# Own buffers for the normed input of the feed-forwards and the second mixer, at chosen byte offsets

## The chip, the cores and the metric

One core of a Trainium2 chip runs the whole program in one launch. The metric is device time in microseconds (us); lower is better.

## What is computed

The reference runs a hybrid block and then two further layers on x of 256 tokens by 1024 features, all in float32:

```
x = x + hybrid_mixer(rmsnorm(x))            # norm 0
x = x + swiglu(rmsnorm(x))                  # norm 2, first feed-forward
x = rmsnorm(x)
x = x + hgrn2_mixer(rmsnorm(x))             # norm 3, second mixer
x = x + swiglu(rmsnorm(x))                  # norm 5, second feed-forward
x = x + rglru_mixer(rmsnorm(x))             # norm 6, third mixer
x = x + swiglu(rmsnorm(x))                  # norm 7, third feed-forward
out = rmsnorm(x)                            # norm 8

swiglu(h) = (silu(h @ w_gate) * (h @ w_up)) @ w_down      # 1024 -> 2816 -> 1024
```

The numbers are those by which the kernel calls its norms (`e`). Norms 1 and 4 are not norms of x: they stand for the inputs of the first two mixers' output products, which have buffers of their own (`eh`, `el`).

## The kernel before, in words

**Weights.** Every weight matrix is cut into units of 1 MB (2048 fp32 columns per partition). SyncE loads units into a ring of three slots, `raw`. ScalarE copies a unit in two halves, rounded, to `whi` (`split`, L983), and VectorE, or GpSimd for the second halves in the feed-forwards, subtracts to get the remainder `wlo` (L1389, L2012). The activations are split in the same way: `hh` and `hl` for a normed input, `gh` and `gl` for the gated product inside a feed-forward, `bh` and `bl` for a branch of the first mixer, `ch` and `cl` in the third mixer. Every product is three matmuls: high by high, low weight by high, high weight by low.

**Two forms of product.** `still` (L507, L510, L515) has a 128x128 block of the weights as stationary operand and 256 columns of the activation, all tokens, as moving operand. It serves `project_columns` and `project_pair`. `moving` (L527, L531, L535) has a 128x128 block of the activation as stationary operand and 512 columns of the weights as moving operand. It serves `project_tokens` and `add_product`. In both forms each matmul has a load of its own stationary block (PEld), and the load for the next matmul runs beside the present one.

**A feed-forward** (`feed_forward(f, e, e2)`) first makes gate and up projections from `hh` and `hl`: 22 units of 48 `still` matmuls, 1056 in all. Two of these units are in `project_pair`, which mixes them with transposes; the rest follow one another. Then `add_product` multiplies `gh`, `gl` by the down weights: 11 units of 24 `moving` matmuls. During its last unit TensorE transposes the next normed input into PSUM (`transposes`, L577), ScalarE copies it to `hh` and VectorE writes the remainder to `hl` (both in functions named `turned`).

**The second mixer** makes 8 `still` units (`hf`, `hq`, 384 matmuls) and then 8 `moving` units (`hv`, `hg`, 24 matmuls each, 192 in all) from `hh` and `hl`, with smaller matmuls of its own between them.

**The order of the work** is written out by hand per engine; every engine waits on semaphores that count what others have finished. A wait is on data, not on a tensor's name.

**Where tensors lie.** Tensors lie one behind the other in a partition in the order of their declarations; stages that follow each other reuse the space behind `gap_stage`. A 128-column stationary block of fp32 is 512 bytes, and all blocks of a tensor begin at a multiple of 512 bytes from the tensor's start. So a tensor's distance from `whi` modulo 512 bytes, called its place here, is the same for all its blocks. From the sizes declared: `whi` and `wlo` have place 0; `hh` and `hl` lie behind `gap_hh` of 32 bytes and have place 32; `eh`, `el` are declared without that gap and have place 0; `gap_stage` brings the stage tensors back to place 0, so `gh` and `gl` have place 0; `gap_bh` gives `bh` and `bl` place 64; `gap_ch` gives `ch` and `cl` place 0.

```
sbuf(root, "gap_hh", [128, 8])
hh = sbuf(root, "hh", [128, 8, 256], f32r)
hl = sbuf(root, "hl", [128, 8, 256], f32r)
```

Of the kernel before, what the change touches and what calls it, by code (L numbers as in the profile page):

```python
# [8 lines left out]
f32 = mybir.dt.float32  # L9
f32r = mybir.dt.float32r  # L10
i32 = mybir.dt.int32
ACT = mybir.ActivationFunctionType
# [62 lines left out]
def build(nc, a):  # L75
    V, A, G, T, S = nc.vector, nc.scalar, nc.gpsimd, nc.tensor, nc.sync
    vq, aq, gq, tq, sq = Waits(V), Waits(A), Waits(G), Waits(T), Waits(S)
    with ExitStack() as root:
# [3 lines left out]
        def sbuf(ctx, name, shape, dt=f32):  # L82
            return ctx.enter_context(nc.sbuf_tensor(name, shape, dt))
# [12 lines left out]
        hh = sbuf(root, "hh", [128, 8, 256], f32r)  # L96
        hl = sbuf(root, "hl", [128, 8, 256], f32r)
# [32 lines left out]
        ffn = []  # L130
        for f in range(3):
            ctx = ExitStack()
            ffn.append((sbuf(ctx, f"gh_{f}", [128, 22, 256], f32r), sbuf(ctx, f"gl_{f}", [128, 22, 256], f32r),
                        sbuf(ctx, f"sg_{f}", [128, 2, 512]), sbuf(ctx, f"bc_f{f}", [128, 256])))
            ctx.close()

        hg = ExitStack()
# [10 lines left out]
        nw = sbuf(hg, "nw", [128, 128])  # L148
        mstat = sbuf(hg, "mstat", [128, 16])
        bc_hg = sbuf(hg, "bc_hg", [128, 256])  # L150
        hg.close()

        lr = ExitStack()
# [10 lines left out]
        bc_lr = sbuf(lr, "bc_lr", [128, 256])  # L164
        gw = sbuf(lr, "gw", [128, 2, 4, 512])
        lr.close()

        def two(ap):
            return ap.rearrange("p (k t) -> p k t", k=2)
# [203 lines left out]
        def bank_of(*key):  # L373
            return banks[turns[key][0]]
# [113 lines left out]
        def tensor_program():  # L488
# [49 lines left out]
            def of_norm(e):  # L538
                return (lambda k: hh_set(e, k)), (lambda k: hl_set(e, k))

            def project_columns(key, e, between=None):
                j = unit_at[key]
                b = turn(("col", *key), next_bank())
                tq.wait_ge(*free(("col", *key)))
                for m in range(units[j][2] // 128):
                    t = still(banks[b][:, 256 * m:256 * m + 256], j, m, hh, hl, range(8), *of_norm(e))
                    if between is not None and m == 0:
                        between()
                t.then_inc(s_full[b], 1)
                used[j, 0] = used[j, 1] = full("col", *key)  # L550

            def project_tokens(key, e, between=None):
                bs = [turn(("tok", *key, 0), next_bank()), turn(("tok", *key, 1), next_bank(), 2)]
                for part in range(2):
                    j = unit_at[(*key, part)]
                    for t in range(2):
                        if part == 0:
                            tq.wait_ge(*free(("tok", *key, t)))
                        tok = moving(banks[bs[t]][:, :], j, t, hh, hl, range(4 * part, 4 * part + 4), 0, 512, *of_norm(e),
                                     first=part == 0, last=part == 1)  # L560
                        if t == 1 or part == 1:
                            tok.then_inc(s_full[bs[t]], 1)
                    b, _, n = turns["tok", *key, 1]
                    used[j, 0] = used[j, 1] = (s_full[b], n - 1 + part)
                    if between is not None:
                        between(part)
# [21 lines left out]
            def project_pair(keys, e):  # L588
                js = [unit_at[key] for key in keys]
                bs = [turn(("col", *key), next_bank(), 2) for key in keys]  # L590
                for part in range(2):
                    for i, j in enumerate(js):
                        for m in range(2):
                            if part == 0:
                                tq.wait_ge(*free(("col", *keys[i])))
                            tok = still(banks[bs[i]][:, 256 * m:256 * m + 256], j, m, hh, hl, range(4 * part, 4 * part + 4),
                                        *of_norm(e), i0=4 * part, first=part == m == 0, last=part == m == 1,
                                        inside=(lambda: spread_factors(e)) if part == i == 1 and m == 0 and e == 3 else None)
                        tok.then_inc(s_full[bs[i]], 1)
                        used[j, part] = (s_full[bs[i]], turns["col", *keys[i]][2] - 1 + part)  # L600
                        if part == i == 0:
                            transposes(1, e)
                        if part == 1 and i == 0 and e != 3:
                            spread_factors(e)
# [367 lines left out]
        def scalar_program():  # L972
# [38 lines left out]
            def turned(c, e):  # L1011
                for n in range(2):
                    q = 2 * c + n
                    aq.wait_ge(*full("tr", e, q))
                    A.activation(hh[:, 2 * q:2 * q + 2, :], two(bank_of("tr", e, q)[:, :]), ACT.Copy).then_inc(s_hh, 1)

            def project_pair(keys, e, bc, evacs):
                j = unit_at[keys[0]]
# [189 lines left out]
            add_product(("wo",), 4, 2)  # L1208

            def feed_forward(f, e, e2, again=None):  # L1210
                gh, gl, sg, bc = ffn[f]

                def gate_of(j):
                    aq.wait_ge(*evac("col", "g", f, j))
                    A.activation(sg[:, j % 2, :], sg[:, j % 2, :], ACT.Silu).then_inc(s_silu, 1)  # L1215

                def up_of(j):
                    aq.wait_ge(*evac("col", "u", f, j))
                    A.activation(gh[:, 2 * j:2 * j + 2, :], two(sg[:, j % 2, :]), ACT.Copy).then_inc(s_gh, 1)  # L1219

                project_pair([("g", f, 0), ("u", f, 0)], e, bc, [lambda: gate_of(0), lambda: up_of(0)])
                for j in range(1, 11):
                    use(("g", f, j))
                    gate_of(j)
                    use(("u", f, j))
                    up_of(j)
                    if f == 0 and j == 2:
                        aq.wait_ge(s_arg, 2)
                        A.activation(cst[:, 1:3, :], cst[:, 1:3, :], ACT.Exp).then_inc(s_exp, 1)
                    if f == 0 and j == 4:  # L1230
                        aq.wait_ge(s_arg, 3)
                        A.activation(cst[:, 0, :], cst[:, 0, :], ACT.Exp).then_inc(s_exp, 1)
                add_product(("down", f), 11, e2, e2 == 8, again=again)
# [143 lines left out]
        def vector_program():  # L1377
# [30 lines left out]
            def turned(c, e):  # L1408
                for n in range(2):
                    q = 2 * c + n  # L1410
                    sl = slice(2 * q, 2 * q + 2)
                    vq.wait_ge(*hh_set(e, 2 * q))
                    V.tensor_tensor(hl[:, sl, :], two(bank_of("tr", e, q)[:, :]), hh[:, sl, :].bitcast(f32),
                                    ALU.subtract).then_inc(evacuated("tr", e, q), 1)

            def spread_factor(e):
# [340 lines left out]
            series = [None]  # L1757

            def feed_forward(f, e, e2, again=None):
                gh, gl, sg, bc = ffn[f]  # L1760

                def gate_of(j):
                    if j >= 2:
                        vq.wait_ge(s_gl, 11 * f + j - 1)
                    scaled(two(sg[:, j % 2, :]), ("g", f, j), e, bc)

                def up_of(j):
                    s = sg[:, j % 2, :]
                    vq.wait_ge(s_silu, 11 * f + j + 1)
                    vq.wait_ge(*full("col", "u", f, j))  # L1770
                    V.tensor_tensor(s, s, bank_of("col", "u", f, j)[:, :], ALU.mult).then_inc(evacuated("col", "u", f, j), 1)  # L1771
                    vq.wait_ge(s_gh, 11 * f + j + 1)
                    V.tensor_tensor(gl[:, 2 * j:2 * j + 2, :], two(s), gh[:, 2 * j:2 * j + 2, :].bitcast(f32), ALU.subtract).then_inc(s_gl, 1)  # L1773

                project_pair([("g", f, 0), ("u", f, 0)], e, [lambda: gate_of(0), lambda: up_of(0)])
                for j in range(1, 11):
                    use(("g", f, j))
                    gate_of(j)
                    use(("u", f, j))
                    up_of(j)  # L1780
                    if f == 0:
                        constants(j)
                if again is not None:
                    vq.wait_ge(*row_ready(3))
                    vq.wait_ge(*row_ready(4))
                    own_row = own.mark(V.tensor_tensor(wrow[:, 0, :], wrow[:, 1, :], wrow[:, 0, :], ALU.mult))
                    vq.wait_ge(*own_row)
                add_product(("down", f), 11, e2, e, e2 == 8, again=again)
# [488 lines left out]
```

## Time and profile before

| | us |
|---|---|
| median of 3 runs (lowest to highest) | 1131.96 (1131.92 to 1132.42) |
| the profiled execution: its time | 1132.61 |
| the profiled execution: its span | 1131.4 |
| TensorE busy, of the span | 1116.7 |
| gate and up projections of one feed-forward, unbroken part | 114.89 |

A busy share of TensorE says that some matmul was in flight, not how fast matmuls follow each other. For that, read start times: the distance between two rows of the timeline, divided by the matmuls between them. It is called the interval below.

### The profile page before, as it was taken

How to read it: one execution, taken by the hardware profiler on the slowest of the kernel's cores; microseconds unless marked ns; L12 is line 12 of the kernel's file. 1: busy time of each engine (PE TensorE's matmuls, PEld its weight loads, DVE VectorE, ACT ScalarE, POOL GpSimd, SP SyncE). 2: the span in 40 equal slices, each digit the busy share in tenths (PEclk: the TensorE clock that was granted, in tenths of full speed). 3: DMA queues.
4: the chain of work that ended last, by engine and by line, in shares of the span. 5: the costliest groups of instructions: out<-in, count | busy, mean ns of one | idle time of the engine just before them, and what ended most of it. 6: DMA issues, size and time to landing. Idle time of an engine off the chain costs nothing.

```text
span 1131.4 us, 19249 instructions
## 1 busy us (share of the span) xinstructions
PE 1116.7 (99%) x8085; PEld 1039.6 (92%) x8085; DVE 658.0 (58%) x1052; ACT 571.3 (51%) x866; POOL 291.6 (26%) x193
## 2 busy tenths in 40 slices
PE   8999999999999999999999999999999999999997
PEld 6899989999989999889998889999889979999986
DVE  6755755677676454338897565343238897434324
ACT  6646555555455644436642545444335855544432
POOL 3022100000005445422311215444510003444440
PEclk9999999999999999999999999999999999999999
DMA  8689474544646666664545358665555254666551
GB/s 266 206 250 335 138 239 150 162 155 137 211 157 208 189 185 203 199 196 142 169 130 169 112 160 274 210 190 190 193 180 188 92 184 151 219 190 188 189 184 38
DMA packets 155088, 207.25 MB, mean 183 GB/s; under 512 B 9471, under 2 KB 128409, under 8 KB 155002
## 3 DMA queue, kind: packets, MB, share of 16 engines
q1 hardware_dynamic: 151274, 193.11, 54.1%
q0 software_dynamic: 3728, 12.92, 3.5%
q8 instruction: 64, 1.05, 0.4%
q14 instruction: 22, 0.18, 0.0%
HBM read 204.78 MB, written 4.24 MB: 185 GB/s over the span
## 4 chain that ended last, share of the span: by engine, by line
PE 81%; DVE 12%; ACT 4%; issue 1%; DMA 1%; POOL 0%; SPq 0%; DVEq 0%; ACTq 0%
PE bank L507 16%; PE bank L510 16%; PE bank L515 16%; PE bank L535 9%; PE bank L531 9%; PE bank L527 9%; DVE wlo L1389 4%; ACT whi L983 1%; PE bank L888 1%; PE bank L802 1%; PE bank L812 1%; DVE area L1537 1%; DMA raw<-in_w_in 1%; PE bank L577 1%; PE bank L824 1%
## 5 line engine op out<-in xcount | busy, mean ns | idle before, releaser
L1389 DVE TENSOR_TENSOR wlo<-raw,whi 128x1024 fp32r<-128x1024 f32 x275 | 336.0, 1249 | 240.0 <-ACT whi L983 239.2
L983 ACT ACTIVATE whi<-raw 128x1024 fp32r<-128x1024 f32 x362 | 360.8, 1045 | 116.0 <-PE bank L535 100.7
L2012 POOL TENSOR_TENSOR wlo<-raw,whi 128x1024 fp32r<-128x1024 f32 x87 | 222.7, 2560 | 250.8 <-ACT whi L983 250.8
L507 PE MATMUL bank<-hh,whi 128*128 128x256 f32 x1784 | 284.3, 281 | 0.0
L515 PE MATMUL bank<-hl,whi 128*128 128x256 f32 x1784 | 281.3, 279 | 0.0
L510 PE MATMUL bank<-hh,wlo 128*128 128x256 f32 x1784 | 281.2, 279 | 0.0
L507 PEld LDWEIGHTS bank<-hh,whi 128*128 128x128 f32 x1784 | 240.6, 188 | 2.1 <-issue 1.4
L510 PEld LDWEIGHTS bank<-hh,wlo 128*128 128x128 f32 x1784 | 239.9, 188 | 0.0
L515 PEld LDWEIGHTS bank<-hl,whi 128*128 128x128 f32 x1784 | 239.7, 188 | 0.0
L2019 POOL TENSOR_TENSOR st<-st,half 128x1 f32<-128x1 f32 x18 | 10.3, 582 | 335.0 <-DVE st L1406 302.1
L527 PE MATMUL bank<-whi,gh 128*128 128x512 f32 x264 | 81.5, 390 | 0.0
L535 PE MATMUL bank<-whi,gl 128*128 128x512 f32 x264 | 81.3, 389 | 0.0
L531 PE MATMUL bank<-wlo,gh 128*128 128x512 f32 x264 | 81.3, 389 | 0.0
L1215 ACT ACTIVATE sg<-sg 128x512 f32<-128x512 f32 x33 | 20.9, 633 | 94.2 <-DVE sg L1436 94.2
L1219 ACT ACTIVATE gh<-sg 128x512 fp32r<-128x512 f32 x33 | 20.8, 632 | 84.1 <-DVE sg L1771 84.1
L535 PEld LDWEIGHTS bank<-whi,gl 128*128 128x128 f32 x264 | 49.6, 188 | 10.4
L531 PEld LDWEIGHTS bank<-wlo,gh 128*128 128x128 f32 x264 | 49.6, 188 | 10.3
L527 PEld LDWEIGHTS bank<-whi,gh 128*128 128x128 f32 x264 | 49.2, 188 | 9.9
L1771 DVE TENSOR_TENSOR sg<-sg,bank 128x512 f32<-128x512 f32 x33 | 22.7, 688 | 55.6 <-PE bank L515 53.5
L1436 DVE TENSOR_TENSOR sg<-bank,bc_f 128x512 f32<-128x512 f32 x33 | 22.8, 690 | 45.4 <-PE bank L515 45.4
L1008 ACT ACTIVATE bank<-x_sb 128x512 f32<-128x512 f32 x26 | 15.6, 600 | 57.7 <-DVE x_sb L1458 29.9
L1773 DVE TENSOR_TENSOR gl<-sg,gh 128x512 fp32r<-128x512 f32 x33 | 30.7, 931 | 23.3 <-ACT gh L1219 23.3
(318 smaller groups left out, 1214.7 us busy)
## 6 DMA issues: line engine op xcount, KB each, us to landing
raw<-in_ffn_w_in SPq DMA_DIRECT2D x88, 512.0 KB, 3.8
raw<-in_w_in SPq DMA_DIRECT2D x72, 512.0 KB, 4.8
raw<-in_ffn_w_out SPq DMA_DIRECT2D x44, 512.0 KB, 3.3
raw<-in_hgrn_w_in SPq DMA_DIRECT2D x32, 512.0 KB, 4.0
raw<-in_w_ffn_gate SPq DMA_DIRECT2D x22, 512.0 KB, 4.4
raw<-in_w_ffn_up SPq DMA_DIRECT2D x22, 512.0 KB, 4.4
raw<-in_w_ffn_down SPq DMA_DIRECT2D x22, 512.0 KB, 3.3
raw<-in_w_branch SPq DMA_DIRECT2D x16, 512.0 KB, 4.4
```

The source lines that it names most:

```text
L507: T.matmul(out, wh[:, i, c], xh[:, k, :], start=first and (i, k) == pairs[0], stop=False)
L510: T.matmul(out, wl[:, i, c], xh[:, k, :], start=False, stop=False)
L515: t = T.matmul(out, wh[:, i, c], xl[:, k, :], start=False, stop=last and (i, k) == pairs[-1])
L527: tok = T.matmul(out, xh[:, k, r], wh[:, i, c], start=first and i == 0, stop=False)
L531: tok = T.matmul(out, xh[:, k, r], wl[:, i, c], start=False, stop=False)
L535: tok = T.matmul(out, xl[:, k, r], wh[:, i, c], start=False, stop=last and i == len(ks) - 1)
L983: A.activation(half_of(whi, j, h), half_of(raw, j, h), ACT.Copy).then_inc(s_hi[j % NS][h], 1)
L1389: V.tensor_tensor(half_of(wlo, j, h), half_of(raw, j, h), half_of(whi, j, h).bitcast(f32), ALU.subtract).then_inc(s_lo[j % NS][h], 1)
L1436: V.tensor_tensor(dst, two(bank_of("col", *key)[:, :]), bc[:, :].rearrange("p (o t) -> p o t", o=1).broadcast_to([128, 2, 256]), ALU.mult) ...
L1771: V.tensor_tensor(s, s, bank_of("col", "u", f, j)[:, :], ALU.mult).then_inc(evacuated("col", "u", f, j), 1)
L1773: V.tensor_tensor(gl[:, 2 * j:2 * j + 2, :], two(s), gh[:, 2 * j:2 * j + 2, :].bitcast(f32), ALU.subtract).then_inc(s_gl, 1)
L2012: G.tensor_tensor(half_of(wlo, j, 1), half_of(raw, j, 1), half_of(whi, j, 1).bitcast(f32), ALU.subtract).then_inc(s_lo[j % NS][1], 1)
```

## The change

Normed inputs 2, 3, 5 and 7 get tensors of their own in place of `hh`, `hl`. `NORMED[e]` names the pair for every norm; norms 0 and 6 keep `hh`, `hl`. `normed_at(t, byte)` takes the high half `byte` bytes behind the tensor's start and the low half 8192 bytes behind that. By the sizes, `normed_f` begins at place 0, so the pairs of the feed-forwards have places 48, 16 and 0; `gap_normed` of 192 bytes gives the second mixer's pair place 0. The readers (`project_columns`, `project_tokens`, `project_pair`) and the two writers (`turned`) go through `NORMED[e]`.

```diff
             ffn.append((sbuf(ctx, f"gh_{f}", [128, 22, 256], f32r), sbuf(ctx, f"gl_{f}", [128, 22, 256], f32r),
-                        sbuf(ctx, f"sg_{f}", [128, 2, 512]), sbuf(ctx, f"bc_f{f}", [128, 256])))
+                        sbuf(ctx, f"sg_{f}", [128, 2, 512]), sbuf(ctx, f"bc_f{f}", [128, 256]),
+                        sbuf(ctx, f"normed_{f}", [128, 4096 + 16], f32r)))
...
         bc_hg = sbuf(hg, "bc_hg", [128, 256])
+        sbuf(hg, "gap_normed", [128, 48])
+        normed_hg = sbuf(hg, "normed_hg", [128, 4096], f32r)
...
+        def normed_at(t, byte):
+            return tuple(t[:, byte // 4 + 2048 * i:byte // 4 + 2048 * i + 2048].rearrange("p (k t) -> p k t", k=8) for i in range(2))
+
+        NORMED = {0: (hh, hl), 2: normed_at(ffn[0][4], 48), 3: normed_at(normed_hg, 0), 5: normed_at(ffn[1][4], 16),
+                  6: (hh, hl), 7: normed_at(ffn[2][4], 0)}
...
-                    t = still(banks[b][:, 256 * m:256 * m + 256], j, m, hh, hl, range(8), *of_norm(e))
+                    t = still(banks[b][:, 256 * m:256 * m + 256], j, m, *NORMED[e], range(8), *of_norm(e))
...
-                        tok = moving(banks[bs[t]][:, :], j, t, hh, hl, range(4 * part, 4 * part + 4), 0, 512, *of_norm(e),
+                        tok = moving(banks[bs[t]][:, :], j, t, *NORMED[e], range(4 * part, 4 * part + 4), 0, 512, *of_norm(e),
...
-                            tok = still(banks[bs[i]][:, 256 * m:256 * m + 256], j, m, hh, hl, range(4 * part, 4 * part + 4),
+                            tok = still(banks[bs[i]][:, 256 * m:256 * m + 256], j, m, *NORMED[e], range(4 * part, 4 * part + 4),
...
-                    A.activation(hh[:, 2 * q:2 * q + 2, :], two(bank_of("tr", e, q)[:, :]), ACT.Copy).then_inc(s_hh, 1)
+                    A.activation(NORMED[e][0][:, 2 * q:2 * q + 2, :], two(bank_of("tr", e, q)[:, :]), ACT.Copy).then_inc(s_hh, 1)
...
-                    V.tensor_tensor(hl[:, sl, :], two(bank_of("tr", e, q)[:, :]), hh[:, sl, :].bitcast(f32),
+                    V.tensor_tensor(NORMED[e][1][:, sl, :], two(bank_of("tr", e, q)[:, :]), NORMED[e][0][:, sl, :].bitcast(f32),
                                     ALU.subtract).then_inc(evacuated("tr", e, q), 1)
```

## Rows read from the trace of the kernel before

**Rows 1.** The page: span, busy time of TensorE, granted clock and GB/s in 40 slices.
```profile
span 1131.4 us, 19249 instructions
PE 1116.7 (99%) x8085; PEld 1039.6 (92%) x8085; DVE 658.0 (58%) x1052; ACT 571.3 (51%) x866; POOL 291.6 (26%) x193
...
PEclk9999999999999999999999999999999999999999
...
GB/s 266 206 250 335 138 239 150 162 155 137 211 157 208 189 185 203 199 196 142 169 130 169 112 160 274 210 190 190 193 180 188 92 184 151 219 190 188 189 184 38
```

**Rows 2.** The page's groups: the three matmuls of `still` on `hh` and `hl`.
```profile
L507 PE MATMUL bank<-hh,whi 128*128 128x256 f32 x1784 | 284.3, 281 | 0.0
L515 PE MATMUL bank<-hl,whi 128*128 128x256 f32 x1784 | 281.3, 279 | 0.0
L510 PE MATMUL bank<-hh,wlo 128*128 128x256 f32 x1784 | 281.2, 279 | 0.0
```

**Rows 3.** Windows, unbroken gate and up stretches of the three feed-forwards; columns named above.
```profile
core 0: us, PE busy (x) PEld busy (x) DVE busy (x) ACT busy (x) POOL busy (x), PEclk, DMA share, GB/s
342.73:457.62 114.89, 114.89 (x988) 114.89 (x987) 57.03 (x77) 60.23 (x71) 54.78 (x22) 1.00 0.64 194
679.24:794.12 114.88, 114.88 (x987) 114.88 (x986) 51.52 (x52) 53.42 (x64) 53.16 (x22) 1.00 0.67 213
950.40:1065.29 114.89, 114.89 (x988) 114.89 (x986) 51.53 (x52) 54.71 (x65) 53.18 (x22) 1.00 0.63 195
```

**Rows 4.** Timeline of PE, first feed-forward: start us, us, instructions; begin and end.
```profile
342.73 0.71 PE L507 MATMUL bank<-hh,whi 128*128 128x256 f32 x4
343.28 0.63 PE L510 MATMUL bank<-hh,wlo 128*128 128x256 f32 x4
...
457.15 0.63 PE L515 MATMUL bank<-hl,whi 128*128 128x256 f32 x4
457.62 0.64 PE L527 MATMUL bank<-whi,gh 128*128 128x512 f32 x2
```

**Rows 5.** Timeline of PE, `moving` with stationary `hh`, `hl` (second mixer).
```profile
604.45 1.17 PE L527 MATMUL bank<-whi,hh 128*128 128x512 f32 x4
605.46 1.09 PE L531 MATMUL bank<-wlo,hh 128*128 128x512 f32 x4
...
609.19 1.10 PE L535 MATMUL bank<-whi,hl 128*128 128x512 f32 x4
610.12 0.60 PE L884 MATMUL bank<-qT,kT 128*128 128x128 f32 x4
```

**Rows 6.** Timeline of PE, `moving` with stationary `gh`, `gl`, second feed-forward (all pairs of two).
```profile
800.04 0.62 PE L531 MATMUL bank<-wlo,gh 128*128 128x512 f32 x2
...
835.40 0.62 PE L531 MATMUL bank<-wlo,gh 128*128 128x512 f32 x2
```

**Rows 7.** Timeline of PE, `still` with moving `bh`, `bl`: third branch, then fourth.
```profile
260.65 0.39 PE L510 MATMUL bank<-bh,wlo 128*128 128x256 f32 x2
...
271.07 0.39 PE L515 MATMUL bank<-bl,whi 128*128 128x256 f32 x2
...
300.02 0.40 PE L510 MATMUL bank<-bh,wlo 128*128 128x256 f32 x2
...
310.15 0.40 PE L515 MATMUL bank<-bl,whi 128*128 128x256 f32 x2
```

**Rows 8.** Timeline of PE: the 64 matmuls of the third mixer's gates, plain fp32.
```profile
878.64 14.08 PE L954 MATMUL bank<-uc,gw 128*128 128x256 f32 x64
892.37 0.82 PE L507 MATMUL bank<-hh,whi 128*128 128x256 f32 x4
```

**Rows 9.** Windows, second mixer: the `still` part, then the `moving` part.
```profile
522.50:576.50 54.00, 53.84 (x455) 53.64 (x452) 47.58 (x89) 35.40 (x43) 21.24 (x33) 1.00 0.49 155
576.50:645.00 68.50, 68.08 (x395) 58.89 (x395) 51.04 (x100) 26.07 (x52) 7.88 (x8) 1.00 0.48 154
```

**Rows 10.** Chain that ended last, second mixer: start us, us, what (longest pieces).
```profile
550.81 2.27 DVE wlo L1389 x2
560.65 1.21 DVE wlo L1389
565.63 2.27 DVE wlo L1389 x2
...
607.48 0.93 PE bank L527 x4
608.42 0.93 PE bank L531 x4
609.35 0.93 PE bank L535 x4
```

More of the change, by code:

```diff
@@ L1210, in feed_forward @@
             def feed_forward(f, e, e2, again=None):
-                gh, gl, sg, bc = ffn[f]
+                gh, gl, sg, bc, _ = ffn[f]
                 def gate_of(j):
@@ L1759, in feed_forward @@
             def feed_forward(f, e, e2, again=None):
-                gh, gl, sg, bc = ffn[f]
+                gh, gl, sg, bc, _ = ffn[f]
                 def gate_of(j):
```

## The prediction

> **What bounds the kernel now.** I read the page first: TensorE is busy for 1116.7 of 1131.4 us, at the full granted clock (2.4 GHz level) in every slice [rows 1]. So time can only come from how fast its matmuls follow each other, or be lost there. The groups show where most of them are: three times 1784 matmuls of one form with the normed input as moving operand [rows 2]. Their mean of 280 ns is flight time and says nothing of pace, so I went to the timeline for intervals. In the first feed-forward 984 `still` matmuls run from 342.73 to 457.62 without a break: 114.89 / 984 = 116.8 ns each [rows 4], and the other two stretches take the same 114.88 and 114.89 us [rows 3]. In them VectorE works 45 to 50%, ScalarE 46 to 52% and GpSimd 46 to 48% of the time, and DMA 63 to 67% [rows 3]: nothing else is near its limit.
>
> **Is 116.8 ns what such a matmul must take?** Two comparisons say no, and both differ from it in where the operands lie. First, the `moving` form: with stationary `hh`, `hl` (place 32) 16 matmuls run from 605.46 to 609.19, 233.1 ns each [rows 5]; with stationary `gh`, `gl` (place 0) 156 run from 800.04 to 835.40, 226.7 ns each [rows 6]. Same form, same moving tensors, same slots; 6.4 ns apart. Second, the `still` form on `bh`, `bl` (place 64), same shape as in the feed-forwards: 92 matmuls from 260.65 to 271.07 are 113.3 ns apart, and 86 from 300.02 to 310.15 are 117.8 ns apart [rows 7]. So one place can give two steady paces, each held to the end of its stretch, with starts that differ in what ran just before.
>
> I read this as two streams out of the same memory, the moving operand and the next stationary block, that get into each other's way as often as their distance and their relative timing make them; a pace once found repeats. In the same trace a plain fp32 product of 256 columns keeps (892.37 - 878.64) / 64 = 214.5 ns [rows 8]. It reads its moving operand for about twice as long, so it is no bound for this form.
>
> The Trainium skill speaks against any effect: "TensorE: Matmul & The Clock Gate", Part 2, step by step, says that TensorE has two independent read ports and that loading the next weights does not take read bandwidth from the running matmul. The trace does not agree: 233.1 against 226.7 ns, with only the stationary tensor changed. By that rule the sum below would be zero.
>
> **The change part by part.**
>
> *Instructions.* None is added, removed or moved: the two writers and three readers get other addresses. ScalarE still makes 4 copies per norm and VectorE 4 subtractions, on the same semaphores. No wait goes either, since the old readers of `hh` were done long before it was written again. No DMA is touched. Cost: nothing, and nothing has to cover it.
>
> *Second mixer, `moving` part.* 8 units of 24, 192 matmuls, go from place 32 to place 0, which is exactly the case of rows 6: 192 x (233.1 - 226.7) = 1.2 us. Here TensorE is the chain in most pieces [rows 10], and VectorE works 51.0 of 68.5 us [rows 9], so I count the whole of it. Bounds: 0, if VectorE's or ScalarE's waits take it up, and 1.2.
>
> *Second mixer, `still` part.* 384 matmuls, place 32 to 0. No row shows `still` at place 0. The nearest is place 64: between -3.5 and +1.0 ns each against 116.8, so -1.3 to +0.4 us. VectorE works 47.6 of 54.0 us there [rows 9] and its `wlo` pieces alternate with TensorE in the chain [rows 10]; what is late next is `wlo`. I take 0.
>
> *The feed-forwards.* 3 x 1056 = 3168 `still` matmuls go from place 32 to 48, 16 and 0. This is the term that decides, and no row shows these places in this form. Lower bound: the pace of 113.3 ns, the quickest of this form, 3.5 ns less per matmul, 3.7 us per feed-forward, 11.1 us in all. Upper bound: 117.8 ns, 1.0 ns more, 1.1 us per feed-forward, 3.3 us in all. I take the lower bound for all three. The reason is rows 5 and 6: place 0 is quicker than 32 in the `moving` form by 6.4 ns, and the `still` form has as moving operand half as many columns; half of 6.4 is 3.2, near the 3.5 between 116.8 and 113.3. For places 48 and 16 that is weaker: they lie between the two seen, and a steady pace halfway, 115.0, would give half the gain there. I do not take halfway because all rows show paces held, not blends.
>
> Is the rest quick enough? A unit would take 48 x 113.3 = 5.44 us in place of 5.60. The down product already uses a 1 MB unit up in 24 x 226.7 = 5.44 us [rows 6], from the same ring, and DMA would have to bring 1 MB in 5.44 us, 193 GB/s, as it does now on average [rows 3], where slices up to 335 GB/s are seen [rows 1]. GpSimd's share, 54.8 us in 114.9, would become 49%. So the cover stands.
>
> *Sum.* 11.1 + 1.2 + 0 = 12.3 us. The profiled execution took 1132.61 us, of which 1131.4 are span and 1.2 lie around it, untouched. That execution stands 0.65 above the median of 1131.96, so the median goes to 1131.96 - 12.3 = **1119.7 us**.
>
> **The rivals.**
>
> *A: all three feed-forwards find the quick pace.* 1119.7. Chance 0.47.
>
> *B: one or two of them do.* Place 64 has both paces in the same trace, so what ran just before a stretch seems to choose [rows 7]. Two quick and one as now: 8.6 us less, 1123.4. One quick, two at 117.8: 3.7 + 1.2 - 2.2 = 2.7 us less, 1129.3. Against it: each stretch starts in the same way, behind the same transposes. Chance 0.25.
>
> *C: place does not matter for these stretches.* This is the skill's rule at work, or paces that depend on timing alone. Then either nothing changes, 1132.0, or only the `moving` part gains, 1130.8. All three at 117.8 belongs here by its size: 3.3 - 1.2 = 2.1 us more, 1134.1. For the rule: three stretches with three different neighbours agree to 0.01 us [rows 3]. Against it: rows 5, 6 and 7. Chance 0.12.
>
> *D: the new places are worse.* Place: the 3168 feed-forward matmuls. If places 16 and 48 put the two streams into step, so that each matmul loses 3 ns more than now, half of what separates rows 5 and 6, the price is 3168 x 3 = 9.5 us, less 1.2: 1140.3. It decides from 117.9 ns on: (117.9 - 116.8) x 3168 = 3.5, less 1.2, is 2.3 us, 0.2% of the time. For it: 117.8 has been seen at another place. Against it: nothing slower is held over a whole stretch in these rows. Chance 0.10.
>
> *E: quicker than any row.* If 16 or 48 parts the two streams altogether, the gain could go beyond 3.5 ns; twice that in two stretches would be 7.4 us more, 1112.3. Chance 0.06.
>
> **How the numbers follow.** 0.2% is 2.3 us, about what a measurement of this kernel can tell from no change. A, B and E lie below 1129.7, though B at its weak end only just: I count 0.77 for faster. C is within 0.2%, with the weak end of B: 0.13. D is slower: 0.10. The range leaves out D and half of E, and takes in A, B and the gaining half of C: 1114 to 1131.
>
> **What would show it.** In the new trace I would divide the three unbroken stretches by 984: 111.5 us for A, 114.9 for C, 116 or more for D. The three need not agree; if they differ, B is right and the place or the start decides. The second mixer's token units should take 24 x 226.7 = 5.44 us in place of 5.67 (604.45 to 610.12, where the next group starts [rows 5]). Shares of the other engines should rise only because the stretch is shorter, and no wait of TensorE for `wlo` or `whi` should appear inside it. The prediction is wrong if places 48 and 16 hold a pace that is neither 113.3 nor near it, or if TensorE starts to wait for the weights' halves at 5.44 us a unit.

## The result and the profile after

The change made the kernel slower: 1137.15 us median of 5 runs (1136.67 to 1137.53), against 1132.06 before (1131.92 to 1132.43). The ratio is 1.0042, 95% interval 1.0031 to 1.0053. Forecast were 1119.7 us and a range of 1114 to 1131.

First the page of the kernel after, its first two lines:

```profile
span 1135.8 us, 19249 instructions
PE 1121.9 (99%) x8085; PEld 1046.4 (92%) x8085; DVE 658.5 (58%) x1052; ACT 571.4 (50%) x866; POOL 291.0 (26%) x193
```

The instructions are as many as before; the span is 4.4 us longer and TensorE is busy for 5.2 us more [rows 1]. Next the windows of the kernel after (columns as in [rows 3]): the three unbroken stretches of gate and up projections, then the second mixer from its first product with the normed input to its last.

```profile
342.48:459.00 116.52, 116.52 (x987) 116.52 (x986) 56.97 (x77) 60.26 (x71) 54.69 (x22) 1.00 0.65 192
680.22:795.10 114.88, 114.88 (x987) 114.88 (x986) 51.53 (x52) 53.42 (x64) 53.47 (x22) 1.00 0.67 213
951.51:1069.67 118.16, 118.16 (x987) 118.16 (x986) 51.57 (x52) 54.65 (x65) 53.38 (x22) 1.00 0.62 189
519.78:642.30 122.52, 122.30 (x850) 114.10 (x849) 101.94 (x193) 60.11 (x89) 26.96 (x39) 1.00 0.51 159
```

The stretches were 114.9 us each [rows 3]. Place 48 now takes 1.6 us more, place 16 nothing more, and place 0 takes 3.3 us more. Divided by 984 matmuls, the paces are 118.4, 116.8 and 120.1 ns. TensorE is busy through the whole of each stretch, the profile lists no wait of it there, and the other engines' busy times stand still: its own pace changed.

The second mixer was 122.99 us (518.45 to 641.44) and is 122.52. In it, one `moving` unit in the timeline of PE, and below it one `still` unit, both of the kernel after; the last two rows are begin and end of that `still` unit in the kernel before:

```profile
605.91 1.17 PE L536 MATMUL bank<-whi,normed_hg 128*128 128x512 f32 x4
606.91 1.07 PE L540 MATMUL bank<-wlo,normed_hg 128*128 128x512 f32 x4
...
610.54 1.07 PE L544 MATMUL bank<-whi,normed_hg 128*128 128x512 f32 x4
611.45 0.60 PE L893 MATMUL bank<-qT,kT 128*128 128x128 f32 x4
...
570.32 0.77 PE L516 MATMUL bank<-normed_hg,whi 128*128 128x256 f32 x4
...
576.20 0.56 PE L897 MATMUL bank<-qT,kT 128*128 128x64 f32 x4
...
568.18 0.77 PE L507 MATMUL bank<-hh,whi 128*128 128x256 f32 x4
...
573.97 0.44 PE L888 MATMUL bank<-qT,kT 128*128 128x64 f32 x3
```

The `moving` unit takes 611.45 - 605.91 = 5.54 us, where it took 5.67 [rows 5]; the `still` unit takes 5.88, where the same one took 5.79. The `moving` units gain about 1.0 us over all eight, and the `still` units give back about 0.9 (46.9 us for their 384 matmuls, 46.0 before), so the two nearly cancel. That the window is 0.5 us shorter comes mostly from two waits of TensorE of 0.2 us each that the kernel before has and the kernel after has not:

```profile
PE bank L585 <- DVE diag L1419: 0.2, 1, 0.2
PE bank L869 <- DVE Ss L1846: 0.2, 1, 0.2
```

They do not follow the place: with the places of before, `e1_place32` below has one of them and `e8_all_moved` neither.

With the pieces ahead of each stretch, from the first projection to the down product, the feed-forwards stand at +1.7 (126.28 from 124.54), +0.1 and +3.4 us (128.01 from 124.59), the second mixer at -0.5. The program's start came 0.4 us earlier. The sum is +4.4 us, the whole difference of the spans.

### The profile page after: what moved, and what is told of

Same layout as the page of the kernel before. It is cut to its first block, busy times and chain, and to the rows that moved or that the text cites. A ratio compares the mean times of both kernels' runs of the same rounds, so it can differ in the third digit from the quotient of the medians.

```text
span 1135.8 us, 19249 instructions
## 1 busy us (share of the span) xinstructions
PE 1121.9 (99%) x8085; PEld 1046.4 (92%) x8085; DVE 658.5 (58%) x1052; ACT 571.4 (50%) x866; POOL 291.0 (26%) x193
## 4 chain that ended last, share of the span: by engine, by line
PE 87%; DVE 8%; ACT 3%; issue 1%; DMA 0%; SPq 0%; POOL 0%; DVEq 0%; ACTq 0%
PE bank L516 18%; PE bank L519 18%; PE bank L524 18%; PE bank L544 9%; PE bank L540 9%; PE bank L536 9%; DVE wlo L1398 3%; PE bank L897 2%; ACT whi L992 1%; PE bank L811 1%; PE bank L821 1%; PE bank L586 1%; DVE area L1546 1%; PE bank L833 1%; DVE uc L1546 0%
## 5 line engine op out<-in xcount | busy, mean ns | idle before, releaser
L516 PE MATMUL bank<-normed,whi 128*128 128x256 f32 x1056 | 168.4, 281 | 0.0
L524 PE MATMUL bank<-normed,whi 128*128 128x256 f32 x1056 | 168.0, 281 | 0.0
L519 PE MATMUL bank<-normed,wlo 128*128 128x256 f32 x1056 | 168.0, 281 | 0.0
L516 PEld LDWEIGHTS bank<-normed,whi 128*128 128x128 f32 x1056 | 143.7, 189 | 0.2
L524 PEld LDWEIGHTS bank<-normed,whi 128*128 128x128 f32 x1056 | 143.4, 189 | 0.0
L519 PEld LDWEIGHTS bank<-normed,wlo 128*128 128x128 f32 x1056 | 143.4, 189 | 0.0
L516 PE MATMUL bank<-hh,whi 128*128 128x256 f32 x600 | 96.5, 283 | 0.0
L519 PE MATMUL bank<-hh,wlo 128*128 128x256 f32 x600 | 94.6, 279 | 0.0
L524 PE MATMUL bank<-hl,whi 128*128 128x256 f32 x600 | 94.5, 279 | 0.0
L516 PEld LDWEIGHTS bank<-hh,whi 128*128 128x128 f32 x600 | 81.2, 188 | 1.8 <-issue 1.4
L519 PEld LDWEIGHTS bank<-hh,wlo 128*128 128x128 f32 x600 | 80.9, 188 | 0.0
L524 PEld LDWEIGHTS bank<-hl,whi 128*128 128x128 f32 x600 | 80.9, 188 | 0.0
```

Source lines behind the costliest of these rows:

```text
L516: T.matmul(out, wh[:, i, c], xh[:, k, :], start=first and (i, k) == pairs[0], stop=False)
L519: T.matmul(out, wl[:, i, c], xh[:, k, :], start=False, stop=False)
L524: t = T.matmul(out, wh[:, i, c], xl[:, k, :], start=False, stop=last and (i, k) == pairs[-1])
```

## The experiments

Theory P, later called D for distance (not rival D of the prediction), says that the place of the normed pair against the weights sets the pace of a stretch. Its rivals are O, it is the buffers' being elsewhere in memory; S, the stage and what ran before it set the pace; and L, the tensor's own alignment counts. In what follows a stretch is one of the three windows above, and its pace is its time divided by 984. Where a run has no ratio, it was executed once, and its windows are what is read.

**1. Same place, own buffers** (`e1_place32`), and **2. places rotated** (`e2_rotated`).

```diff
-        NORMED = {0: (hh, hl), 2: normed_at(ffn[0][4], 48), 3: normed_at(normed_hg, 0), 5: normed_at(ffn[1][4], 16),
-                  6: (hh, hl), 7: normed_at(ffn[2][4], 0)}
+        NORMED = {0: (hh, hl), 2: normed_at(ffn[0][4], 32), 3: normed_at(normed_hg, 32), 5: normed_at(ffn[1][4], 32),
+                  6: (hh, hl), 7: normed_at(ffn[2][4], 32)}
```

In the second the four numbers are 0, 16, 48 and 16, in the same order. (In all runs of this kind `normed_f` and `normed_hg` are made 1024 bytes longer than a pair, to leave room.)

> All four pairs keep their own buffers but lie at place 32, as hh and hl do. Theory P (the place of the normed pair against the weights sets the pace of a stretch): the three unbroken stretches are 116.8 ns a matmul again (114.9 us each), the second mixer as before, time 1132.0 us. Rival O (it is the buffers being elsewhere in memory, not the place): stretches stay at 118.4, 116.8 and 120.1 ns, time 1137.1 us.

> Places 0, 48 and 16 in the first, second and third feed-forward, 16 in the second mixer. Theory P: paces follow the places, 120.1, 118.4 and 116.8 ns (118.2, 116.5 and 114.9 us). Rival S (what ran before a stretch and which stage it is set the pace): 118.4, 116.8 and 120.1 ns stay where they are. For place 16 in the second mixer nothing is known in the form with the pair as stationary operand; P expects something between the 226.7 ns of place 0 and the 233.1 ns of place 32.

The windows of the first run, then of the second:

```profile
342.70:457.59 114.89, 114.89 (x988) 114.89 (x986) 56.95 (x77) 60.22 (x71) 54.74 (x22) 1.00 0.65 194
679.31:794.20 114.89, 114.89 (x987) 114.89 (x986) 51.49 (x52) 53.42 (x64) 53.17 (x22) 1.00 0.68 213
950.42:1065.31 114.89, 114.89 (x987) 114.89 (x986) 51.51 (x52) 54.70 (x65) 53.15 (x22) 1.00 0.63 195
```

```profile
342.46:460.61 118.15, 118.15 (x987) 118.15 (x986) 57.00 (x77) 60.21 (x71) 54.81 (x22) 1.00 0.64 189
682.21:798.73 116.52, 116.52 (x988) 116.52 (x986) 51.53 (x52) 53.45 (x64) 53.13 (x22) 1.00 0.67 210
955.11:1070.00 114.89, 114.89 (x988) 114.89 (x987) 51.54 (x52) 54.68 (x65) 53.49 (x22) 1.00 0.63 194
```

With place 32 everywhere the kernel takes 1132.37 us, ratio 0.9999 (0.9989 to 1.0008): rival O falls for place 32. With the places rotated the stretches go with them, 118.2, 116.5 and 114.9 us (1137.33 us for the whole): rival S falls for these places. Place 16 gave 233.3 ns in seven units of the `moving` part, as place 32 did, and 226.6 in one: two paces, nothing between.

**3. Places 64 and 128, 256, 96** (`e3_place64`: 64 in all four; `e4_scan`: 128, 256, 256, 96 in the order of `NORMED`).

> Place 64 everywhere, where bh gave 113.3 and 117.8 ns. P with two paces at one place: each of the three stretches is 111.5 us (113.3 ns) or 115.9 us (117.8 ns), none in between. If places repeat every 64 bytes, 64 acts as 0: 120.1 ns, 118.2 us in all three. Time 1121 to 1134 us in the first case, about 1142 us in the second.

> Places 128, 256 and 96 in the three feed-forwards, 256 in the second mixer. If the pattern repeats every 64 bytes: 120.1, 120.1 and 116.8 ns. If it repeats every 128 bytes: 120.1, 120.1, and 96 is open. If every 256: the first is open, the second 120.1. If only every 512: all three open. O and S expect 118.4, 116.8 and 120.1 ns.

The first stretch of each:

```profile
342.54:458.51 115.97, 115.97 (x987) 115.97 (x986) 57.01 (x77) 60.25 (x71) 54.86 (x22) 1.00 0.65 192
```

```profile
343.31:461.47 118.16, 118.16 (x988) 118.16 (x986) 56.99 (x77) 60.25 (x71) 54.78 (x22) 1.00 0.63 189
```

At 64 all three stretches took 116.0 us, 117.9 ns; none found the 113.3 that two stretches of `bh` had [rows 7]. So 64 is not 0, and a repeat every 64 bytes is out. Places 128, 256 and 96 gave 118.16 us each here, as 0 did; experiment 7 has 128 at another pace. Times: 1135.80 and 1142.84 us.

**4. Everything moved by 96 bytes** (`e8_all_moved`), on the kernel before.

```diff
+        sbuf(root, "gap_all", [128, 24])
         whi = sbuf(root, "whi", [128, NS, UC], f32r)
```

> The kernel before with a gap of 96 bytes ahead of whi, so that weights, normed inputs and all that follows lie 96 bytes further on and every place against the weights is as before. Theory D (the distance between the moving stream and the next stationary block counts): nothing changes, 1132.0 us and 114.9 us for each stretch. Rival L (the tensor's own alignment to some line of memory counts): the normed input goes from 32 to 128 bytes against where the tensors begin, and the stretches go to another pace, up to 120.1 ns or 118.2 us each; the `moving` products on gh change from 226.7 ns too.

```profile
342.88:457.76 114.88, 114.88 (x987) 114.88 (x986) 57.01 (x77) 60.22 (x71) 54.83 (x22) 1.00 0.64 195
679.47:794.36 114.89, 114.89 (x988) 114.89 (x986) 51.49 (x52) 53.41 (x64) 53.27 (x22) 1.00 0.68 213
950.60:1065.48 114.88, 114.88 (x987) 114.88 (x986) 51.49 (x52) 54.69 (x65) 53.30 (x22) 1.00 0.63 195
```

The stretches are as before, the `gh` products run at 226.7 ns, and the time is 1132.80 us. Rival L falls for alignments to 64 bytes and more: there the distance between the two operands counts. Since 96 is a multiple of 32, an alignment to 32 bytes or less stays untested.

**5. The other places** (`e5_scan`: 80, 96, 112, 24; `e6_scan`: 40, 112, 56, 72; `e7_scan`: 88, 48, 104, 8; the second number is the mixer's).

> Places 80, 112 and 24 in the feed-forwards, 96 in the second mixer. Theory D with a repeat every 128 bytes (0, 128 and 256 all gave 120.1 ns): 24 lies between 16 and 32, which gave 116.8 each, so 116.8; 80 lies between 64 (117.9) and 96 (120.1), so 118 to 120; 112 lies between 96 and 128 (both 120.1), so 120.1. The second mixer's first part at 96: 120 ns as in the third feed-forward of the run before. A pace under 116 at any place would be a version to take.

> Places 40, 56 and 72 in the feed-forwards, 112 in the second mixer. By neighbours: 40 between 116.8 and 118.4, 56 between 117.9 and 118.4, 72 at 117.9 or above. If the pace has steps of 16 bytes, 40 is as 32 (116.8), 56 as 48 (118.4), 72 as 64 (117.9). For the second mixer's part with the pair as stationary operand at 112, D says that the distance is that of place 16 seen from the other side, so it need not be 226.7 ns; 233.4 if only place 0 is quick.

> Places 88, 104 and 8 in the feed-forwards, 48 in the second mixer. With steps of 16 bytes: 88 as 80, 104 as 96 (120.1), 8 as 0 (120.1). Without steps: 8 between 120.1 and 116.8. The second mixer's stationary part at 48: 233.4 ns as at 16, 32 and 64.

The windows of the run with 80, 112 and 24:

```profile
343.08:461.24 118.16, 118.16 (x987) 118.16 (x986) 56.93 (x77) 60.25 (x71) 54.74 (x22) 1.00 0.63 189
683.29:794.91 111.62, 111.62 (x988) 111.62 (x987) 51.60 (x52) 53.49 (x64) 53.82 (x22) 1.00 0.69 219
951.37:1069.53 118.16, 118.16 (x987) 118.16 (x986) 51.52 (x52) 54.69 (x65) 53.46 (x22) 1.00 0.61 190
```

I had expected 112 to be slow, like its neighbours 96 and 128. It gave 111.62 us, 113.4 ns. The other eight stretches were 118.2 us, 120.1 ns, so there is no going by neighbours: 24 lies between 16 and 32 and is as slow as 0. In the second mixer, 112 made the `still` part quicker (45.0 us for its 384 matmuls, 46.0 before) and left the `moving` part at 233.2 ns; 96 gave 234.3 there, 48 gave 233.3. Times: 1136.86, 1142.86 and 1142.76 us.

**6. All four at 112** (`e10_place112`).

> The change with all four places at 112. Place 112 gave 113.4 ns in the second feed-forward (111.62 us against 114.89) and took 0.9 us off the second mixer's first part. Theory D (place alone): three stretches of 111.6 us, 3 x 3.27 = 9.8 us, and 1.0 us in the second mixer: 10.8 us less than the kernel before, 1121.4 us. Rival S (112 was quick for what ran before it, as bh at 64 was in two stretches of five): one or two stretches at 111.6 us, the others above 116; time 1125 to 1131 us.

```profile
342.27:453.89 111.62, 111.62 (x987) 111.62 (x986) 57.24 (x77) 60.33 (x71) 55.48 (x22) 1.00 0.67 200
675.31:786.93 111.62, 111.62 (x987) 111.62 (x986) 51.59 (x52) 53.51 (x64) 53.75 (x22) 1.00 0.69 219
942.91:1054.53 111.62, 111.62 (x987) 111.62 (x986) 51.60 (x52) 54.79 (x65) 53.80 (x22) 1.00 0.64 200
```

The time is 1121.85 us, ratio 0.9910 (0.9895 to 0.9924), 0.4 us off what theory D gave. The weights and the other engines keep up at 5.44 us a unit.

**7. A longer gap in place of buffers** (`e9_hh112`, and `e11_hh112_bh112` with `gap_bh` of 28 too): a miss that told something.

```diff
-        sbuf(root, "gap_hh", [128, 8])
+        sbuf(root, "gap_hh", [128, 28])
...
-        sbuf(root, "gap_stage", [128, 80])
+        sbuf(root, "gap_stage", [128, 60])
```

> The kernel before without any new buffer: gap_hh goes from 32 to 112 bytes, and gap_stage is shortened so that all else keeps its place. D: as above, and the first and third mixers gain too, 384 x 3.3 ns = 1.3 us in the third, and up to 1464 x 3.5 ns = 5 us in the first where TensorE sets the pace there: 1115 to 1120 us. If own buffers are needed: 1132.0 us.

> The run before with bh and bl at 112 in place of 64 too. D: the branches' 384 matmuls, 45.1 us, go to 113.4 ns each with their starts: 1.0 to 1.5 us less than the run before.

The times are 1147.48 us, ratio 1.0134 (1.0119 to 1.0149), and 1146.76 us, 1.0129 (1.0112 to 1.0146). The program's addresses say why: in it a tensor begins at a multiple of 32 bytes, so `hh` lay at 128, `gh` at 32 and `bh` at 96, in the second run at 160. The timeline of PE in the first run's down product shows what `gh` at 32 costs, the two rows after it are begin and end of a `moving` unit on `hh` at 128, and the last two, of the second run, are those of the 96 matmuls of a branch at 160:

```profile
480.13 0.63 PE L527 MATMUL bank<-whi,gh 128*128 128x512 f32 x2
...
506.73 0.63 PE L527 MATMUL bank<-whi,gh 128*128 128x512 f32 x2
...
619.59 1.17 PE L527 MATMUL bank<-whi,hh 128*128 128x512 f32 x4
...
625.26 1.00 PE L888 MATMUL bank<-qT,kT 128*128 128x64 f32 x8
...
301.84 0.40 PE L507 MATMUL bank<-bh,whi 128*128 128x256 f32 x2
...
313.11 0.61 PE L527 MATMUL bank<-whi,eh 128*128 128x512 f32 x2
```

57 pairs lie between the first two rows: 26.60 / 114 = 233.3 ns, what [rows 5] has for `hh` at 32, where [rows 6] has 226.7 for `gh` at 0. `bh` at 96 ran at 120 ns. `hh` at 128 ran at 120.0 in the broken pieces ahead of the first two stretches, but at 118.7 in all three stretches, in both runs, where `e4_scan` had 120.1 at the same place in a buffer elsewhere: another place with two paces, and one at which rival O is not ruled out. The first of the three:

```profile
346.50:463.34 116.84, 116.84 (x988) 116.84 (x986) 56.91 (x77) 60.25 (x71) 54.49 (x22) 1.00 0.64 191
```

These runs also speak against a repeat every 128 bytes. The `moving` unit at 128 takes 625.26 - 619.59 = 5.67 us, as at 32, where at 0 it takes 5.54; the units settle at 232 to 233.4 ns, not at 226.7. The branch at 160, 128 bytes behind 32, took 11.27 / 96 = 117.4 ns, and the five branch stretches settled between 117.3 and 118.8, none at the 116.7 of place 32.

**8. `hh` and `hl` truly at 112, no new buffers** (`e12_hh112`), and **`bh`, `bl` too** (`e13_hh112_bh112`).

```diff
-        sbuf(root, "gap_hh", [128, 8])
-        hh = sbuf(root, "hh", [128, 8, 256], f32r)
-        hl = sbuf(root, "hl", [128, 8, 256], f32r)
+        normed = sbuf(root, "normed", [128, 28 + 4096], f32r)
+        hh, hl = (normed[:, 28 + 2048 * i:28 + 2048 * i + 2048].rearrange("p (k t) -> p k t", k=8) for i in range(2))
...
-        sbuf(root, "gap_stage", [128, 80])
+        sbuf(root, "gap_stage", [128, 56])
```

The second also makes `bh`, `bl` slices that begin 48 bytes into a tensor at place 64.

> The kernel before with hh and hl as slices of one tensor, 112 bytes behind its start, so that they do lie at place 112 in every stage (in the run with a longer gap_hh the tensors had been set to the next multiple of 32 bytes: hh at 128, gh at 32, bh at 96). gap_stage is shortened, all else keeps its place. D: stretches of 111.6 us, the second mixer's first part as in the run with four places at 112, and more in the first mixer (1464 matmuls at 116.7 to 120 go to 113.4: up to 5 us) and the third (384 x 3.3 ns = 1.3 us): 1115 to 1120.5 us. Rival B (own buffers are needed, since the run with the longer gap was slower): 1132 us or more.

> The run before with bh and bl at place 112 in the same way, in place of 64, where three of five stretches kept 117.8 ns and two 113.3. D: all five keep 113.4 ns, 240 x 4.4 ns = 1.0 us less than the run before. If what ran ahead chooses the pace at 112 too, some stay at 117 to 118.

The fourth branch in the timeline of PE, first run, then second run, then `e2_rotated` (96 matmuls from its first row to the row of `eh`):

```profile
295.80 0.40 PE L506 MATMUL bank<-bh,whi 128*128 128x256 f32 x2
...
307.11 0.62 PE L526 MATMUL bank<-whi,eh 128*128 128x512 f32 x2
```

```profile
294.59 0.39 PE L506 MATMUL bank<-branch_in,whi 128*128 128x256 f32 x2
...
305.47 0.62 PE L526 MATMUL bank<-whi,eh 128*128 128x512 f32 x2
```

```profile
299.04 0.39 PE L516 MATMUL bank<-bh,whi 128*128 128x256 f32 x2
...
309.92 0.39 PE L536 MATMUL bank<-whi,eh 128*128 128x512 f32 x1
```

The times are 1118.57 us, ratio 0.9881 (0.9866 to 0.9896), and 1116.95 us, 0.9869 (0.9852 to 0.9885), with all stretches at 111.6 us in both. In the first run all five branch stretches, still at 64, kept 117.8 ns, the two that had been quick before among them: 11.31 / 96 for the one shown. For those two, what ran ahead of them had changed its pace, not they. The branch shown is another matter: it kept 113.3 ns in `e2_rotated`, `e3_place64` and `e14_around112` and 117.8 in the other runs that have `hh` at 32 and `bh` at 64, although the program is the same up to there in all but `e8_all_moved`, where all lies 96 bytes further on. So at place 64 something smaller than the program can choose the pace. At 112 all five kept about 113.3 (10.88 / 96), and that gave 1.6 us, more than the 1.0 expected because five were slow and not three. The second of these kernels beats both that the study began with.

**9. Around 112** (`e14_around112`: 108, 104, 116, 120).

> How wide the quick place is: 108, 116 and 120 in the three feed-forwards, 104 in the second mixer. If places count in steps of 16 bytes, 116 and 120 act as 112 (113.4 ns, 111.6 us) and 108 and 104 as 96 (120.1 ns, 118.2 us). If the quick place is 112 alone, all are near 120.1 ns, as 104 was.

```profile
342.17:460.35 118.18, 118.18 (x988) 118.18 (x987) 56.90 (x77) 60.13 (x71) 54.40 (x22) 1.00 0.63 189
682.88:803.49 120.61, 120.61 (x988) 120.61 (x986) 51.38 (x52) 53.45 (x64) 52.94 (x22) 1.00 0.64 203
959.92:1079.19 119.27, 119.27 (x988) 119.27 (x986) 51.52 (x52) 54.76 (x65) 53.14 (x22) 1.00 0.61 188
```

The paces are 120.1, 122.6 and 121.2 ns, the time 1146.49 us: the quick place is narrow, and 4 bytes behind it lies the slowest pace of all. That all places within a step of 16 bytes act alike is out. But each of the ten places tried that is not a multiple of 16 bytes took 120.1 ns or more in its stretch, and `whi` began at a multiple of 16 in every run. So for those places the distance is not told apart from an alignment of the pair itself to 16 bytes; no run tests it.

All places seen, in ns: stretches by their time divided by 984, short pieces and `moving` units once they are steady.

| place | `still` (pair is moving operand) | `moving` (pair is stationary operand) |
|---|---|---|
| 0, 256 | 120.1 | 226.7 |
| 128 | 120.1, 118.7 | 232 to 233.4 |
| 16 | 116.8, in short pieces also 118.7 | 233.3, one unit 226.6 |
| 32 | 116.8, in short pieces also 117.8, in one piece 120.0 | 233.3 |
| 48 | 118.4 | 233.3 |
| 64 | 117.9, in short pieces also 113.3 | 233.5 |
| 96 | 120.1 | 234.3 |
| 112 | 113.4 | 233.2 |
| 116 | 122.6 | |
| 120 | 121.2 | |
| 8, 56, 80 | 120.1, in a short piece also 118.3 to 118.4 | |
| 72 | 120.1, in short pieces 121.6 | |
| 24, 40, 88, 108 | 120.1 | |
| 160 | in short pieces 117.3 to 118.8 | |
| 104 | 120.1 | 233.4 |

## Why the prediction was wrong

**The bound and the kind of term were right.** TensorE's pace was the only thing that moved; no instruction or wait was added, and the other engines hid nothing and cost nothing. Which operands lie where does set the pace, and at place 0 by the size I had worked with, about 3.3 ns a matmul, but upwards.

**The step that failed** is in the feed-forward term: "place 0 is quicker than 32 in the `moving` form by 6.4 ns, and the `still` form has as moving operand half as many columns; half of 6.4 is 3.2". The pace at a place does not carry over from one form to the other, and no row had shown `still` at any of the three places. At 0 the `moving` form is at its quickest, 226.7, and the `still` form at its usual slow pace, 120.1. At 112 it is the other way round, 233.2 and 113.4. The number I meant to support, 113.3, did exist; the place for it was 112. Each feed-forward was put down at -3.7 us; they came out at +1.7 (48), +0.1 (16) and +3.4 (0).

A figure of the Trainium skill shows the flaw from another side. "TensorE: Matmul & The Clock Gate", section "Back-to-back issue gap", gives about N / 2.4 + 2.5 ns for the isolated gap of one matmul of N columns, and says that for large N a sustained stream comes out below it. As estimates from that formula, 256 columns take 109.2 ns and 512 take 215.8; the runs here lie above both. Against these estimates place 0 costs 10.9 ns a matmul in both forms, and 32 costs 7.6 in one and 17.5 in the other. A cost per matmul is not halved with the columns, and its order over places is a matter of the form.

**The bounds were too narrow.** I took 113.3 and 117.8 as ends because place 64 showed them. The paces go from 113.4 to 122.6. Two values at one place were a warning that the nearest row does not bound a place never seen; the range had to reach at least as far up as rival D.

**Points that held.** One is the place-0 term of the second mixer's `moving` part: 226.7 ns was reached and about 1.0 of the 1.2 us came, since each unit starts slower and needs its first dozen matmuls to settle. The other is the reserve of the other engines: units of 5.44 us were sustained in the runs at 112. The thought behind rival B, that what ran before chooses, is in part right: at 64 and, in short pieces, at 32 one place had several paces, and at 64 some changed with what ran ahead and one without any change in the program; at 16, 48 and 112 one pace ruled in each of the unbroken stretches seen.

**Points that failed beside it.** For the mixer's `still` part 0 was forecast, between -1.3 and +0.4; it cost 0.9, outside the bound. Rival D had the direction and the price, 3 ns a matmul, but placed it at 16 and 48; it came at 0 in full and at 48 by half, and 16 was as before. Rival C falls: with the same instructions the pace went from 113.4 to 122.6 ns by place alone. The rule of the Trainium skill that the prediction names beside it, two independent read ports ("TensorE: Matmul & The Clock Gate", Part 2, step by step), would leave the pace as it was; the runs do not agree.

**What stays open.** That the other stream is the load of the next stationary block is an inference: moving both operands together changes nothing in the stretches, and moving either one against the other does, but no run took the load away. Why 112 is quick, whether the pair's own alignment to 16 bytes counts beside the distance, and what in the start of a stretch picks one of two paces, was not found.

## What to carry to other kernels

Where TensorE is the bound, read the interval of its matmuls over a long unbroken stretch, and compare it between products of the same shape: a difference with no wait in it can be the place of the two operands in memory. Here it was worth 1.3% of the time (1116.95 us against 1131.85 in the same round). Find the place by trying, form by form, since neither neighbours nor the other form foretell it. Put the offset inside a tensor, by slicing, and look at the addresses that the program really has.

## What the runs showed of the hardware

The pace of fp32r matmuls of 256 columns went from 113.4 to 122.6 ns by the place of the moving operand against the weights alone, 8%, at a granted clock of 1.00 throughout. Places 0 and 256 gave the same in both forms (120.1 and 226.7 ns), so a repeat every 256 bytes fits; 128 did not (118.7 in six stretches, 232 to 233.4 in the `moving` form), so a repeat every 128 bytes does not. Single steps of 4 bytes matter (112: 113.4; 116: 122.6). After the start, a pace is kept to the end of a stretch of 984 matmuls, and one place can hold two of them (64: 113.3 and 117.9; 128: 118.7 and 120.1). The `moving` form settled at about 226.7 or at 232 to 234.3, in no run between.
